# Cross-attention norms: value projection first, and Sqrt with a reciprocal in place of Ln and Exp

## The reference

```python
def memory_cross_attention(h, m, w_cq, w_ckv, qn, kn, w_co):
    q = rms_norm((h @ w_cq).reshape(B, S, X_HEADS, X_DH), qn)      # S 512, 4 heads of 64
    kv = (m @ w_ckv).reshape(B, M, 2, X_HEADS, X_DH)               # M 256
    k = rms_norm(kv[:, :, 0], kn)
    v = kv[:, :, 1]
    logits = jnp.einsum('bshd,bmhd->bhsm', q, k).astype(jnp.float32) * (X_DH ** -0.5)
    p = jax.nn.softmax(logits, axis=-1)
    o = jnp.einsum('bhsm,bmhd->bshd', p.astype(v.dtype), v).reshape(B, S, X_HEADS * X_DH)
    return o @ w_co

def rms_norm(x, g):
    y = xf * lax.rsqrt(jnp.mean(xf * xf, axis=-1, keepdims=True) + NORM_EPS)
    return (y * g.astype(jnp.float32)).astype(x.dtype)
```

## Time and profile before

| | |
|---|---|
| median of 3 runs | 1812.97 us (1808.01 to 1813.9) |
| profiled execution | 1808.01 us, its span 1805.8 us |
| mean granted TensorE clock | 0.925 of full |
| TensorE matmul busy | 1606.6 us, 89% |
| VectorE busy | 1174.4 us, 65% |
| ScalarE busy | 785.6 us, 44% |
| GpSimd busy | 437.5 us, 24% |

### The profile page before, as it was taken

The page is one execution under the profiler, slowest core; times in us unless marked ns, Lnnn a source line. Parts: engine busy times, 40 slices in busy tenths (PEclk is TensorE's granted clock), DMA queues, the critical chain, the costliest instruction groups (busy, mean ns, idle before and its releaser), DMA issues. The chain is left out here.

```text
span 1805.8 us, 19167 instructions
## 1 busy us (share of the span) xinstructions
PE 1606.6 (89%) x6326; PEld 1041.2 (58%) x6326; DVE 1174.4 (65%) x1734; ACT 785.6 (44%) x1161; POOL 437.5 (24%) x210
## 2 busy tenths in 40 slices
PE   6999999999885999999479999999998769999991
PEld 2445555544564787887334445554455658787881
DVE  2494377533246999999435943984422579999984
ACT  2512132250253777777123221322503447777750
POOL 0000122100001565655300001221000025565643
PEclk9999999799986999999779999997998769999996
DMA  5231301050313999998711420011302159999974
GB/s 178 97 59 69 117 1 48 1 165 0 140 42 125 358 390 399 397 397 328 261 37 36 93 70 1 1 47 35 130 27 113 47 193 358 399 396 399 397 299 163
DMA packets 152935, 307.55 MB, mean 170 GB/s; under 512 B 35062, under 2 KB 48284, under 8 KB 152748
## 3 DMA queue, kind: packets, MB, share of 16 engines
q1 hardware_dynamic: 141180, 264.18, 41.0%
q0 software_dynamic: 6912, 25.17, 3.8%
q10 hardware_dynamic: 4784, 17.45, 2.4%
HBM read 280.02 MB, written 27.93 MB: 171 GB/s over the span
## 5 line engine op out<-in xcount | busy, mean ns | idle before, releaser
L526 PE MATMUL ps<-hT,arena 128*128 128x512 f32 (+2 forms) x768 | 358.2, 618 | 1.6 <-DVE hT L868 1.6
L1620 POOL TENSOR_TENSOR rest_w_down<-arena,head_w_down 128x2048 fp32r<-128x2048 f32 x32 | 217.0, 6780 | 137.0 <-ACT head_w_down L1707 137.0
L526 PEld LDWEIGHTS ps<-hT,arena 128*128 128x128 f32 (+2 forms) x768 | 140.1, 188 | 187.5 <-issue 181.5
L1765 DVE TENSOR_TENSOR rest_w_down<-arena,head_w_down 128x2048 fp32r<-128x2048 f32 x32 | 159.7, 4991 | 6.7 <-ACT head_w_down L1707 6.7
L1765 DVE TENSOR_TENSOR rest_w_up<-arena,head_w_up 128x2048 fp32r<-128x2048 f32 x64 | 143.4, 2280 | 1.3 <-ACT head_w_up L1707 1.3
L1652 PE MATMUL ps<-head_w_gate,xg_head 128*128 128x512 f32 x256 | 107.4, 420 | 33.0 <-DVE xg_rest L1771 33.0
L1765 DVE TENSOR_TENSOR rest_w_gate<-arena,head_w_gate 128x2048 fp32r<-128x2048 f32 x60 | 134.6, 2284 | 0.6 <-issue 0.6
L1707 ACT ACTIVATE head_w_up<-arena 128x2048 fp32r<-128x2048 f32 x64 | 120.6, 1964 | 0.0
L1707 ACT ACTIVATE head_w_down<-arena 128x2048 fp32r<-128x2048 f32 x64 | 118.9, 1912 | 1.2 <-issue 1.2
L1652 PE MATMUL ps<-head_w_down,he_head 128*128 128x512 f32 x256 | 104.2, 407 | 15.8 <-POOL rest_w_down L1620 15.8
L923 DVE CUSTOM_DVE_ANT_0 scratch<-ps,scratch 128x128 f32<-128x128 f32 (+3 forms) x48 | 23.6, 491 | 141.5 <-PE ps L640 91.2
(11 more groups left out here) (279 smaller groups left out, 3058.3 us busy)
## 6 DMA issues: line engine op xcount, KB each, us to landing
arena<-in_w_gate SPq DMA_DIRECT2D x64, 1024.0 KB, 8.4
arena<-in_w_up SPq DMA_DIRECT2D x64, 1024.0 KB, 7.8
arena<-in_w_down SPq DMA_DIRECT2D x64, 1024.0 KB, 7.3
yrows<-yb ACTq DMA_DIRECT2D x32, 512.0 KB, 6.4
arena<-in_w_in SPq DMA_DIRECT2D x10, 1536.0 KB, 6.7
arena<-in_w_in SPq DMA_DIRECT2D x4, 2048.0 KB, 8.3
arena<-in_w_in SPq DMA_DIRECT2D x20, 256.0 KB, 5.1
arena<-in_w_out SPq DMA_DIRECT2D x2, 2048.0 KB, 8.4
```

The costliest lines, as they stand in the source:

```text
L526: last = nc.tensor.matmul(ps[n % 2][0:width, :], w[:, c, col:col + width], hT[:, c, :], start=(c == 0), stop=(c == KD - 1))
L1620: nc.gpsimd.tensor_tensor(wl[2][:, c, :], raw[2][:, c, :], wh[2][:, c, :].bitcast(F32), ALU.subtract)\
L1765: nc.vector.tensor_tensor(wl[q][:, c, :], raw[q][:, c, :], wh[q][:, c, :].bitcast(F32), ALU.subtract)\
```

## The change

The value projection is issued before the query projection, with its own count of cp_done, so the counts are now keys, values, query half, query half. Each head sum follows its projection. ScalarE makes the root in one pass (Sqrt), between the squares, and copies the values after the keys' square. VectorE takes the reciprocal of each root in place, 128x512, before the product with projection and gain.

```diff
                     last.then_inc(sN["cp_done"], 1)
                     rows_turned(XM + NT - 1, 6)
+                    for i in range(2):
+                        for c in range(KD):
+                            last = nc.tensor.matmul(ps[5][:, 256 * i:256 * i + 256], memT[:, c, P * i:P * i + P],
+                                                    wckv[:, c, 256:512], start=(c == 0), stop=(c == KD - 1))
+                    last.then_inc(sN["cp_done"], 1)
...
                         last.then_inc(sN["cp_done"], 1)
-                        if i:
-                            head_sums(0)
-                            head_sums(1)
-                    for i in range(2):
-                        for c in range(KD):
-                            last = nc.tensor.matmul(ps[5][:, 256 * i:256 * i + 256], memT[:, c, P * i:P * i + P],
-                                                    wckv[:, c, 256:512], start=(c == 0), stop=(c == KD - 1))
-                            if i == 0 and c == 1:
-                                head_sums(2)
-                    last.then_inc(sN["cp_done"], 1)
+                        head_sums(i)
+                    head_sums(2)
...
                     def head_squares(n, src):
-                        act.wait_ge(sN["cp_done"], n + 1)
+                        act.wait_ge(sN["cp_done"], 1 if n == 0 else n + 2)
...
-                    for n in range(3):
-                        head_squares(n, ps[(4, 2, 3)[n]])
-                    for n in range(3):
+                    def head_roots(n):
                         act.wait_ge(sN["cn_sum"], n + 1)
-                        do(nc.scalar.activation(wide[n], ps[X_SUMS[n]], ACT.Ln, bias=epst[:, :], scale=1.0 / XD), wait=False)
-                    lns = count[ca_]
-                    for n in range(3):
-                        act.wait_ge(ca_, lns - 2 + n)
-                        do(nc.scalar.activation(wide[n], wide[n], ACT.Exp, scale=-0.5), "cn_root", wait=False)
-                    act.wait_ge(sN["cp_done"], 4)
+                        do(nc.scalar.activation(wide[n], ps[X_SUMS[n]], ACT.Sqrt, bias=epst[:, :], scale=1.0 / XD), "cn_root", wait=False)
+
+                    head_squares(0, ps[4])
+                    act.wait_ge(sN["cp_done"], 2)
                     do(nc.scalar.activation(cv, ps[5].rearrange("p (i n) -> p i n", i=2), ACT.Copy), "cp_out", wait=False)
+                    head_squares(1, ps[2])
+                    head_roots(0)
+                    head_squares(2, ps[3])
+                    head_roots(1)
+                    head_roots(2)
...
                         dve.wait_ge(sN["cn_root"], n + 1)
+                        do(V.reciprocal(wide[n], wide[n]))
                         do(V.scalar_tensor_tensor(dst, src, pc("cqn" if n else "ckn"), wide[n], ALU.mult, ALU.mult), "cn_done")
```

## The result

The changed kernel takes 1826.45 us (median of 6 runs, 1824.84 to 1829.5), the kernel before 1813.35 (6 runs). The ratio is 1.0080, 95% interval 1.0064 to 1.0095: 0.8% slower. The forecast was 1824.8 us, with a range of 1811 to 1834 and a chance of 0.63 for "slower".

A forecast was written before the change was run, and what follows sets the result against it. The prediction took the value projection and its copy to end last before the first logits. Reciprocals 4.98 plus clock 0.95 gave 5.93 per layer, 11.9 for two, on a median of 1812.97: 1824.8 us, range 1811 to 1834.

The forecast's parts named there:

- the formula: Start of layer one's first logits: 488.21 plus two exposed VectorE reciprocals, against 488.33 before; 2r - 0.12 us per layer.
- r: Time of one 128x512 reciprocal on VectorE, taken as 2.55 us.
- the disputed term: Two exposed 128x512 reciprocals on VectorE ahead of the first logits, 4.98 us per layer at 2.55 each.
- the bounds 0.45 and 4.08: Limits in us for one 128x512 reciprocal: cheap as the fastest multiplication form, or 7.7 ns per element.
- the likeliest case: Middle reciprocal on VectorE, between about 1.4 and 3.4 us each: 1820 to 1829 us in all, chance 0.45.
- Per layer ahead of the logits: Delay of the first logits by the exposed reciprocals, without the clock term: 4.98 us per layer.
- The clock: First logits on TensorE run at half clock after the longer hole, 2.08 instead of 1.13: 0.95 us more per layer.
- Costs of nothing: Value copy off the path, keys' reciprocal hidden on idle VectorE, returning 1.28 us table load hidden before the softmax's exponentials.
- Cheap reciprocal: Rival: VectorE's reciprocal costs as little as a multiplication, about 0.7 us; 1815.6 to 1817.4 us, chance 0.32.
- Upper reciprocal: Rival: VectorE's 128x512 reciprocal takes 4.08 us, 18.0 us in all, 1831 us; chance 0.18.
- Faster through the clock: Rival: TensorE's clock stays full through the softmax, at most 4.9 us per layer back; 1805.7 us, chance 0.05.
- the move of the values: Value projection ahead of the queries fills TensorE's hole, whose sum shrinks by 1.14 us.

The follow-up runs named there:

- e4: Changed kernel with the queries' reciprocals and products cut by tile of 128 tokens, only tile 0 ahead of the first logits; 1820.24 us, ratio 1.0054 to before.
- e8: Changed kernel with nine unread products filling TensorE's hole between last head sum and first logits; 1825.19 us, ratio 1.0065 to before.
- e3: Changed kernel with a multiplication by 1.0 in place of each reciprocal, a probe of time only; 1815.3 us, ratio 1.0003 to before.
- e9: Kernel before with early head sums, values last in bank 7, Ln and Exp, plus idle products in the softmax's holes; 1804.58 us, ratio 0.9959.
- e1: Changed kernel's order alone, with Ln and Exp as before and no reciprocal; 1819.02 us, ratio 1.0047 to before.
- e7: Kernel before with head sums issued early, values still last but in bank 7, Ln and Exp kept; 1807.37 us, ratio 0.9975.
- e10: Second run of the kernel before with early head sums, values last in bank 7, Ln and Exp; 1806.7 us, ratio 0.9965.

## Why the prediction held, and where it was off

- **What ends last, and the formula.** Shown. The prediction put the logits at 488.21 + 2r; with r = 3.35 that is 494.91, measured 494.42. Its steps each came 0.2 to 0.4 us early: queries 469.61 for 469.84, head sum 1 at 484.20 for 484.54, last Sqrt 486.21 for 486.62. I had started the value projection at the end of the transposes, where its matmuls follow 0.23 sooner, and had paced the queries with 13.84 us, which held the start-up of one projection.
- **The reciprocal, the disputed term, was mis-sized:** 3.35 us, where 2.55 was taken; the bounds 0.45 and 4.08 held it.

```profile
L1419 DVE RECIPROCAL rs<-rs x4: 3352/3353/3354, 478.3 to 1393.8; 128x512 f32<-128x512 f32 x4
```

  It lies at the upper edge of the likeliest case (r up to 3.4). With e4's sizes the cost is 0.153 + 0.00625 us per element. That gives the 178 ns at four elements in the earlier trace rows exactly, so the information was there. The error was to take the difference of two tiny reciprocals, 164 and 178, of which the first varies from 152 to 165 by line. Taking the cheapest simple operation of one element, 153 (L925), as the fixed part of the 178 would have given (178 - 153) / 4 = 6.25 ns and r = 3.35. That is said with the result at hand; these runs show it for one operation. The Trainium skill ("VectorE: DVE Perf Modes", section "Walkthrough: the 8-slice pipeline in each mode") gives the reciprocal a repeat count of 8. The runs don't bear it out as eight cycles per element: at the 0.96 GHz of that page (section "Specifications") the measured slope is six.
- **Per layer ahead of the logits:** 4.98 forecast, 6.15 measured. The reciprocals add 1.6 to the forecast, the early steps take 0.4 off.
- **The clock:** 0.95 per layer forecast, 0.46 measured against the mean of before. The first logits did take 2.08 us. Windows of half a microsecond show that the granted clock was half from 3.6 us ahead of them to 10 us behind their start, in both layers. In the two traces of before it was half from about 2.7 to 13 us behind that start in three layers, and to 16.1 in layer one of the first trace, which has the highest value, 46.53. So the low stretch came earlier in the work: it took in the first logits and ended sooner behind them. Against the three other layers (45.52) the cost is 0.7, as in e8. The forecast, which took the rest of the stretch as moved along with the work, was too high by 0.25 to 0.5. Two windows of the changed kernel:

```profile
488.00:492.00 4.00, 0.00 (x0) 0.00 (x0) 3.93 (x3) 0.20 (x1) 0.00 (x0) 0.83 0.00 0
...
504.00:508.00 4.00, 2.21 (x25) 1.59 (x24) 0.99 (x3) 3.12 (x10) 0.00 (x0) 0.96 0.00 0
```

- **Sum:** 5.93 per layer forecast, 6.6 measured; 11.9 against 13.1 in all. The reciprocal alone was 1.6 too low per layer, the early steps and the clock took 0.9 off again. With r = 3.35 the prediction's own sum would have given 1828.0, so the closeness of 1824.8 to 1826.45 is in part luck; the mechanism is not. A slip of one microsecond: the upper end of the likeliest case (r = 3.4) adds up to 1828, not 1829.
- **Costs of nothing:** the value copy, the first reciprocal and the table load were hidden, as said.
- **Rivals.** Cheap reciprocal: its time is e3's, and the row of L1419 rules it out. Upper reciprocal: r is 3.35, not 4.08. Faster through the clock: the clock fell at about 490.6 (0.83 in the window from 488), as before, and e9 shows 1.4 to 2 us per layer where the prediction bounded it by 4.9; even a full clock could not have repaid 6.15.
- **What the prediction didn't say:** it named the move of the values as a saving of 1.14 us and not as a loss of cover. Its formula held that loss, for it charged the whole norm chain behind the queries, but gave it no number of its own. The runs do: in the new order the chain left bare costs 3.05 us per layer with Ln and Exp (e1), 0.30 with Sqrt and a multiplication (e3) and 6.15 with Sqrt and the reciprocal.

## What to carry to other kernels

Independent work behind a chain is its cover. Before moving such a block forward into a hole, compare the hole (1.14 us here) with the chain that is left bare behind it (the changed kernel's 8.24 us wait); a small piece of the chain itself, here a head sum, fills the hole better. For an operation seen only in tiny sizes, work out its fixed part from the cheapest simple operation of one element too (here it would have met 3.35; this is one case), and keep the range as wide as the two estimates differ. Compare traces by durations between the same two instructions: the one ahead of the logits repeated to 0.01 us, the one behind them only to about 1.4 (e7 and e10), while whole executions of one kernel differed by up to 17 us (1804.33 to 1821.25 in the 35 runs of before).

## What the runs showed of the hardware

A float32 reciprocal on VectorE costs 953, 1754 and 3353 ns for 128, 256 and 512 elements per partition, where the multiplication takes 430 ns for 512. TensorE's granted clock fell from 2.4 to 1.2 GHz around the first logits, from 3.8 us ahead of their start to 5.2 behind it, in both layers of every kernel but e9. In the first trace of before it fell about 2.4 us behind their start, in the hole of 3.55 us that follows 1.13 us of work; in the changed kernel it fell inside the hole of 8.24 us. With the holes of the softmax filled by idle products it stayed full, for a gain of about 1.4 us per layer against the same order without them (e9 against e7 and e10). Code that no edit touched took 813.9 to 822.1 us over twelve traces, with low-clock windows at different places; that I had not expected of a single core, and it bounds what a median of few runs can tell here.
